# Two more adaLN blocks inside the GLA mixer, unread matmuls in PE's gaps, and jumps ahead of the last waits

## The reference

```
for i in range(4):
    sh1, sc1, g1, sh2, sc2, g2 = split(silu(cond) @ w_ada[i] + b_ada[i], 6)      # adaLN, per group
    h = rmsnorm(x) * (1 + sc1) + sh1
    x = x + g1 * mixer_i(h)     # 0: Hyena (long convolution by DFT), 1: gated linear attention (GLA),
                                # 2: FNet (2-D DFT and a linear map), 3: PoolFormer (window means)
    h = rmsnorm(x) * (1 + sc2) + sh2
    x = x + g2 * moe(h)         # top-1 group of 4, then top-2 of its 4 SwiGLU experts; 16 experts
y = rmsnorm(x)                  # also an output: the final GLA states of the context tokens
```

## Time and profile before

| | |
|---|---|
| median of 3 runs (lowest to highest) | 1424.62 us (1424.25 to 1424.86) |
| profiled execution | 1424.48 us |
| its span, first to last instruction | 1422.3 us |
| PE busy | 1358.9 us, 96% |
| DVE, ACT busy | 360.7 us, 281.8 us |
| read from HBM | 548.98 MB |
| mean granted clock of PE | 0.992 of full speed |
| chain that ended last | PE 83%, DMA 13%, DVE 2%, ACT 1% |

### The profile page before, as it was taken

The page is one execution under the profiler, slowest core; times in us unless marked ns, Lnnn a source line. Parts: engine busy times, 40 slices in busy tenths (PEclk is TensorE's granted clock), DMA queues, the critical chain, the costliest instruction groups (busy, mean ns, idle before and its releaser), DMA issues.

```text
span 1422.3 us, 17398 instructions
## 1 busy us (share of the span) xinstructions
PE 1358.9 (96%) x7294; PEld 748.3 (53%) x7294; DVE 360.7 (25%) x881; ACT 281.8 (20%) x511; POOL 32.1 (2%) x30
## 2 busy tenths in 40 slices
PE   7999999999989999999999989999998898999986
PEld 3786585444435788774444436744443365444433
DVE  3434514111113303323111112331111153111113
ACT  3211024111103221232111104421111053111101
POOL 0001310000000000010000000100000000000000
PEclk9999999999999999999999999999999997999999
DMA  9955999999999993499999999999999999999993
GB/s 382 420 191 214 403 416 394 428 426 428 428 425 421 421 376 102 172 413 403 429 428 426 429 423 420 421 426 428 427 427 428 424 421 425 426 428 428 427 426 153
DMA packets 55076, 552.27 MB, mean 388 GB/s; under 512 B 6033, under 2 KB 8017, under 8 KB 8913
## 3 DMA queue, kind: packets, MB, share of 16 engines
q1 hardware_dynamic: 53360, 549.09, 92.5%
q10 hardware_dynamic: 1634, 2.01, 0.4%
HBM read 548.98 MB, written 2.10 MB: 387 GB/s over the span
## 4 chain that ended last, share of the span: by engine, by line
PE 83%; DMA 13%; DVE 2%; ACT 1%; SPq 0%; issue 0%; POOL 0%; DVEq 0%; POOLq 0%
PE bank L737 26%; PE bank L683 14%; PE bank L761 13%; DMA ring<-in_moe_w 10%; PE bank L643 5%; PE bank L702 5%; PE bank L720 3%; PE bank L514 2%; PE bank L531 2%; DMA ring<-in_pool_w 2%; PE bank L657 2%; PE bank L968 1%; PE bank L860 1%; PE bank L593 1%; PE bank L589 1%; PE bank L744 1%
## 5 line engine op out<-in xcount | busy, mean ns | idle before, releaser
L737 PE MATMUL bank<-ring,arena 128*64 128x512 f32 x896 | 200.4, 595 | 28.1 <-DMA ring<-in_moe_w 26.5
L737 PE MATMUL bank<-ring,hT 128*64 128x512 f32 x1024 | 225.3, 594 | 0.0
L761 PE MATMUL bank<-ring,arena 128*64 128x512 f32 x896 | 198.7, 596 | 0.6 <-DMA ring<-in_moe_w 0.6
L737 PEld LDWEIGHTS bank<-ring,arena 128*64 128x64 f32 x896 | 63.7, 137 | 157.6 <-issue 131.5
L737 PEld LDWEIGHTS bank<-ring,hT 128*64 128x64 f32 x1024 | 72.1, 137 | 139.4 <-issue 137.3
L1447 DVE TENSOR_TENSOR rows<-rows,bank 128x512 f32<-128x512 f32 x32 | 22.0, 688 | 463.6 <-PE bank L737 463.6
L761 PEld LDWEIGHTS bank<-ring,arena 128*64 128x64 f32 x896 | 61.6, 137 | 117.8 <-issue 114.6
L683 PE MATMUL bank<-hT,ring 128*128 128x256 f32 x512 | 112.4, 380 | 0.0
L683 PEld LDWEIGHTS bank<-hT,ring 128*128 128x128 f32 x512 | 96.5, 190 | 15.2 <-issue 2.5
L1167 ACT ACTIVATE yv_big<-bank,arena 128x512 fp32r<-128x512 f32 x64 | 44.0, 688 | 285.5 <-PE bank L761 285.5
L1466 DVE SCALAR_TENSOR_TENSOR yv_rest<-bank,arena,yv_big 128x512 fp32r<-128x512 f32 x64 | 48.1, 751 | 200.6 <-ACT yv_big L1167 200.6
(11 more groups left out here) (217 smaller groups left out, 1281.7 us busy)
## 6 DMA issues: line engine op xcount, KB each, us to landing
ring<-in_moe_w SPq DMA_DIRECT2D x152, 2048.0 KB, 20.4
ring<-in_w_ada SPq DMA_DIRECT2D x96, 1024.0 KB, 22.0
ring<-in_moe_w SPq DMA_DIRECT2D x48, 1024.0 KB, 26.8
arena<-in_moe_w SPq DMA_DIRECT2D x16, 1024.0 KB, 19.6
arena<-in_moe_w SPq DMA_DIRECT2D x8, 2048.0 KB, 11.8
ring<-in_hy_w_in SPq DMA_DIRECT2D x12, 1024.0 KB, 27.3
ring<-in_hy_w_out SPq DMA_DIRECT2D x4, 1024.0 KB, 12.3
ring<-in_gla_w_v SPq DMA_DIRECT2D x4, 1024.0 KB, 22.8
```

The costliest lines, as they stand in the source:

```text
L737: last = mm(bank[4 + kind][SLOTS * e:SLOTS * e + SLOTS, :], x[:, k, at:at + SLOTS], w[:, kk, e, :], start=k == 0, stop=k == KD - 1)
L761: last = mm(bank[6 + q // 2][SLOTS * e:SLOTS * e + SLOTS, :], hidT[:, f, SLOTS * e:SLOTS * e + SLOTS], w[:, ff, e, :], start=f == 0, stop= ...
```

## The change

Blocks 7 and 8 join 5 and 6 inside GLA, between the pieces of the v map, and block 9 takes the place of 7 there; block 10 becomes the one beside layer 1's end, and block 11 is multiplied in FNet. The end of layer 2 and the pool mixer then have no block. Their gaps get `keep_running`: matmuls with `ones` as weights into a PSUM bank of which nobody reads what they write. Such matmuls stand at the start of the kernel too. The loads in `piece_stream` are reordered to match. Three of ACT's four first loads are issued later, behind the first norm's root. The output is stored in four parts instead of two, and SP and ACT jump over `far_rounds` before the last waits and stores. Everything that the reference asks for is still computed. The diff, with little context:

```diff
@@ -125,10 +125,10 @@
     before = [ada(0) + pieces("w_in", 12) + ada(1) + ada(2) + ada(3) + pieces("w_out", 4) + ada(4),
-              ada(5, 0, 5) + pieces("wq", 2) + ada(5, 5) + pieces("wk", 2) + ada(6) + pieces("wv", 4)
-              + pieces("wg", 4) + ada(7) + pieces("wo", 4) + ada(8),
-              ada(9) + pieces("fn", 4) + ada(10),
-              ada(11, 0, 5) + pieces("pool", 1) + ada(11, 5)]
+              ada(5, 0, 5) + pieces("wq", 2) + ada(5, 5) + pieces("wk", 2) + ada(6) + pieces("wv", 2) + ada(7)
+              + pieces("wv", 4)[2:] + ada(8) + pieces("wg", 4) + ada(9) + pieces("wo", 4) + ada(10),
+              ada(11) + pieces("fn", 4),
+              pieces("pool", 1)]
     out, at = [], 0
@@ -467,11 +467,6 @@
-            sp.wait_ge(s("out_ready"), 4)
-            sp.dma_start(a["y"][:, 0:4], hT[:, 0:4]).then_inc(s("stored"), 16)
-            sp.wait_ge(s("state_stored"), 32)
-            sp.wait_ge(s("stored"), 16 * 2)
             def one_round(b, i):
@@ -487,6 +482,11 @@
             far_rounds(sp, "sp", reg, one_round)
+            sp.wait_ge(s("state_stored"), 32)
+            for k in (0, 4):
+                sp.wait_ge(s("out_ready"), k + 2)
+                sp.dma_start(a["y"][:, k:k + 2], hT[:, k:k + 2]).then_inc(s("stored"), 16)
+            sp.wait_ge(s("stored"), 16 * 4)
@@ -522,6 +522,12 @@
             for c in range(4):
+                if c == 1:
+                    ada_turned(6)
+                if c == 2:
+                    ada(7, 0, 8)
+                if c == 3:
+                    ada_turned(7)
                 w8 = arrived(("wv", c), KD)
@@ -532,13 +538,14 @@
                         last.then_inc(s("gla_proj"), 1)
-            ada_turned(6)
+            ada(8, 0, 8)
             gates(pe, 1)
+            ada_turned(8)
             pe.wait_ge(s("v_ready"), 4)
...
-                pe.wait_ge(s("mod_ready"), 7)
+                pe.wait_ge(s("mod_ready"), 9)
                 for m in range(first, end):
@@ -599,7 +606,7 @@
             pe.wait_ge(s("g_raw"), 8)
-            ada(7, 0, 3)
+            ada(9, 0, 3)
@@ -609,8 +616,8 @@
                     last.then_inc(s("osum_mm"), 1)
-            ada(7, 3, 8)
-            residual(1, "wo", oT, lambda k: pe.wait_ge(s("o_ready"), k + 1), turned=7, beside=8)
+            ada(9, 3, 8)
+            residual(1, "wo", oT, lambda k: pe.wait_ge(s("o_ready"), k + 1), turned=9, beside=10)
@@ -852,8 +859,18 @@
+            wide_ones = ones[:, 0:1].broadcast_to([P, 512])
+            def keep_running(times, x, b=7):
+                for _ in range(times):
+                    mm(bank[b][:, 0:x.shape[1]], ones[:], x)
             def moe(i, beside=None):
                 pe.wait_ge(s("rw_loaded"), 16 * (i + 1))
+                if beside is None:
+                    pe.wait_ge(s("mod_ready"), ADAS)
+                    keep_running(2, wide_ones)
                 for k in range(KD):
@@ -876,6 +893,8 @@
                     ada(beside, 6, 7)
+                else:
+                    keep_running(3, wide_ones)
                 pe.wait_ge(s("members"), i + 1)
@@ -885,6 +904,8 @@
                     ada(beside, 7, 8)
+                else:
+                    keep_running(1, wide_ones)
                 pe.wait_ge(s("htok_rest"), 4 * (i + 1))
@@ -906,8 +927,11 @@
+            pe.wait_ge(s("cond_ready"), 1)
+            keep_running(2, ones[:], 0)
             pe.wait_ge(s("filter_loaded"), 16)
             mm(bank[5][0:HY_HID, 0:L], fsmall[0:HY_EMB, 1, 0:HY_HID], fsmall[0:HY_EMB, 0, :]).then_inc(s("f_mm"), 1)
+            keep_running(12, ones[:], 0)
             pe.wait_ge(s("cond_ready"), 3)
@@ -915,6 +939,7 @@
             last.then_inc(s("f_mm"), 1)
+            keep_running(3, ones[:], 0)
             norm(0)
@@ -1010,12 +1035,12 @@
             pe_gla(pe, arrived, ada, ada_turned, norm, h_ready, project, residual)
-            moe(1, 8)
-            ada(9, 0, 2)
+            moe(1, 10)
+            ada(11, 0, 2)
             norm(4)
-            ada(9, 2, 5)
+            ada(11, 2, 5)
             pe.wait_ge(s("cm_loaded"), 16 * 2)
@@ -1030,7 +1055,7 @@
                     last.then_inc(s("mix_mm"), 1)
-            ada(9, 5, 8)
+            ada(11, 5, 8)
             pe.wait_ge(s("mix_rows"), 8)
@@ -1040,15 +1065,14 @@
                     last.then_inc(s("mix_mm"), 1)
-            ada_turned(9)
+            ada_turned(11)
             pe.wait_ge(s("mix_rows"), 8 + 4)
-            residual(2, "fn", rhs=fnm, beside=10)
-            moe(2, 10)
-            ada(11, 0, 2)
+            residual(2, "fn", rhs=fnm)
+            moe(2)
             norm(6)
-            ada(11, 2, 5)
+            keep_running(2, wide_ones)
             pw = arrived(("pool", 0), KD)
@@ -1061,14 +1085,12 @@
                         last.then_inc(s("mix_mm"), 1)
-            ada(11, 5, 8)
             pe.wait_ge(s("mix_rows"), 12 + 4)
...
                 last.then_inc(s("res_mm"), 1)
-            ada_turned(11)
             norm(7)
@@ -1094,10 +1116,7 @@
-            act.dma_start(base[:], a["c_base"]).then_inc(s("base_loaded"), 16)
-            act.dma_start(ar(19472, 3 * P), a["c_masks"]).then_inc(s("masks_loaded"), 16)
             act.dma_start(skip_row[0:1], a["skip"]).then_inc(s("skip_loaded"), 16)
-            act.dma_start(rw[:], a["router"][0]).then_inc(s("rw_loaded"), 16)
@@ -1232,6 +1251,9 @@
             inverse_root(0)
+            act.dma_start(base[:], a["c_base"]).then_inc(s("base_loaded"), 16)
+            act.dma_start(ar(19472, 3 * P), a["c_masks"]).then_inc(s("masks_loaded"), 16)
+            act.dma_start(rw[:], a["router"][0]).then_inc(s("rw_loaded"), 16)
             for c in range(10):
@@ -1362,9 +1384,10 @@
-            act.wait_ge(s("out_ready"), 8)
-            act.dma_start(a["y"][:, 4:8], hT[:, 4:8]).then_inc(s("stored"), 16)
             far_rounds(act, "act", reg, one_round)
+            for k in (2, 6):
+                act.wait_ge(s("out_ready"), k + 2)
+                act.dma_start(a["y"][:, k:k + 2], hT[:, k:k + 2]).then_inc(s("stored"), 16)
@@ -1764,8 +1787,9 @@
             v.memset(sc[:], 0.0).then_inc(s("sc_clear"), 1)
-            ada_rows(6)
-            ada_mod(6)
+            for n in (6, 7, 8):
+                ada_rows(n)
+                ada_mod(n)
             scores(0)
@@ -1786,15 +1810,15 @@
                 tt(o, o, ors[:, m // 2], ALU.mult).then_inc(s("o_ready"), 1)
-            ada_rows(7)
+            ada_rows(9)
             residual(1, g1(1))
-            ada_mod(7)
-            moe(1, 8)
+            ada_mod(9)
+            moe(1, 10)
             norm(4)
-            ada_rows(9)
+            ada_rows(11)
             residual(2, g1(2))
-            ada_mod(9)
-            moe(2, 10)
+            ada_mod(11)
+            moe(2)
             norm(6)
@@ -1802,14 +1826,12 @@
             chain(tt(xT[:], xT[:], gb.unsqueeze(3).broadcast_to([P, KD, G, L]), ALU.add))
-            ada_rows(11)
             for m in range(KD):
...
                 last.then_inc(s("x_added"), 1)
-            ada_mod(11)
             moe(3)
```

## The result

Four executions of the changed kernel took 1412.62 to 1415.59 us, median **1413.8 us**; the kernel before took 1424.74 us beside it (1424.25 to 1425.24). The ratio is 0.9923, 95% interval 0.9908 to 0.9938: faster by 0.8%. The forecast was 1413.5 us. Of the terms behind it some were wrong and cancelled, so the stages come first. From here on "the changed kernel" is the one of the diff.

A forecast was written before the change was run, and what follows sets the result against it. PE, busy for 96% of the span, sets the end with its few idle stretches. Terms -3.3 + 15.3 - 1.3 - 6.5 - 8.7 - 3.4 - 3.2 = -11.1 from 1424.6 give 1413.5 us, range 1406 to 1420.5.

The forecast's parts named there:

- GLA: Gated mixer: two more blocks, their turnings and a new modulation wait, no wait for loads; +15.3 us.
- a granted clock of under 1.00 behind the pool mixer: Layer 3: named as a sign that the forecast is wrong; clock forecast at 1.00 in every window behind 12 us.
- a wait of PE for a load between 500 and 545: In GLA: PE idling on loads there was named as a sign of being wrong; 0 to 2 us possible, 0 taken.
- Start: First norm: unread products raise the clock (-2.4), three loads leave the queue ahead of x (-0.9); sum -3.3 us.
- Layer 2: Mixer and routing chain of layer 2: block work leaves, mostly from gaps; -1.3 us.
- MoE 2 and 3: Expert stages of layers 2 and 3: eight fewer loads ahead, longer lead; -6.5, and -3.4 plus -1.9 for layer 3's first gathers.
- (d): Removed loads do not shorten the MoEs, as SP's ordered queue hands the lead back; 1423.4 us, 8 in 100.
- (e): The MoE tails vanish altogether, 201.2 and 200.9 instead of 205.0 twice, a further -8; 1405.5 us, 8 in 100.
- Layer 3: Layer 3's mixer and routing: block 11 leaves and the clock is kept; -8.7 us, of which -1.9 is the first gathers.
- Rival (b): The clock still falls in the last routing chain, layer 3, costing 4.9 us; 1418.4 us, 11 in 100.
- Rival (c): Unread products hold the clock nowhere; layer 2's chain and the pool mixer fall too; 1434 us, 5 in 100.
- End: Last stores: jump moved into SP's idle time (2.5 us), store of half the size (-0.7); sum -3.2 us.

The follow-up runs named there:

- e5: The changed kernel once more, unaltered: median 1413.49 us, ratio 0.9923 to the kernel before.
- e4: The changed kernel with base, masks and router loaded ahead of x again, as in the kernel before: 1415.42 us, ratio 0.9934.
- e6: The changed kernel with only one block more in GLA instead of two, block 11 back in layer 2's end and beside its experts: 1413.35 us, ratio 0.9917.
- e8: The changed kernel with eight expert slabs of layer 2 queued ahead of the first w2 loads: 1415.66 us, ratio 0.9936.
- e1: The kernel before with only the adaLN blocks moved, no unread products, old start and end: 1430.91 us, ratio 1.0041.
- e3: The changed kernel without the unread products of layers 2 and 3, those of the start kept: 1423.83 us, ratio 0.9992.
- e11: The changed kernel without the two unread products behind norm(6), ahead of the pool mixer: 1414.45 us, ratio 0.9925.
- e2: The kernel before with only the new start (unread products, later loads) and new end (jumps, four stores), no block moved: 1418.33 us, ratio 0.9952.
- e7: The changed kernel with block 11's pieces only where PE waits, replacing layer 2's unread products: 1411.8 us, ratio 0.9899.
- e9: e7 plus three half-width unread products in layer 3's bare gaps: 1409.7 us, ratio 0.9889.
- e12: The changed kernel without the 17 unread products of the start, the three loads still behind x: 1414.8 us, ratio 0.9921.

## Why the forecast held

That the sum came within 0.3 us of the median is partly luck. The stages fell by 9.7 us in the profiled execution and by 12.6 in e5, for a forecast of 11.1: GLA's +1.1 and layer 3's +2.1 were made up for by the two MoEs (-1.2 and -0.8), and layer 3 alone moves by 2.6 us from one execution to the next. Two things that the prediction named as signs of being wrong came true: a granted clock of under 1.00 behind the pool mixer, and a wait of PE for a load between 500 and 545. Both were small, 2.6 and 0.4 us.

**Start.** Right in sum (-3.3; -3.2 in the profiled execution, -2.6 in another), wrong in its parts. "I take -0.9, bounds 0 and -1.0" for the loads: x came 2.2 us earlier, outside the bounds, so the size over the full rate (0.43 MB at 424 GB/s) is not what these small loads cost there. Why is not shown; in before the engines moved 134 to 380 GB/s at first, until near 6 us. (The rule of the Trainium skill that the prediction cites, "DMA: Bandwidth & Descriptors", section "Issuing engines are not separate DMA queues", agrees in kind: loads of ScalarE's queue do delay those of SyncE's. It gives no price for it.) "-2.4" for the clock: 2.0 by itself (e4), and about 1.0 remains once x is early, since the unread products stand in PE's order ahead of x.

**GLA.** +15.3, measured +16.4: two blocks at 7.0 and 7.7 (0.4 of it the wait for the last piece, where "0 to 2 us of waiting; I take 0" was the forecast), two turnings 0.9, and 0.3 for the modulation; the last 0.5 I can't place.

**Layer 2.** -1.3, measured -1.1.

**MoE 2 and 3.** -6.5 and -5.3, measured -7.7 and -6.1. The mechanism, eight loads fewer and so a longer lead capped by the ring, is shown by e6 (eight loads back: MoE 2 219.2 us, 218.7 before) and e8 (a longer lead is of no use). The forecast lead, 33 us, was met. The cap is at 204.2 rather than 205.0. Rivals (d) and (e) are out: PE still waits 18.2 us for slabs over the four stages (26.5 before), 6.1 us in the first and 3.6 to 4.5 in each of the others.

**Layer 3.** -6.8; -4.7 in the profiled execution, -7.3 in e5 (from the norm's sum to the first expert product 19.4 and 16.8 us, forecast 17 to 18). Rival (b), the clock falls all the same, happened in part: the mean clock shows it in three of ten executions, and in the profiled one it lasted 6.8 us and cost 2.6 instead of 4.9 us, as it was over before the gathers. "So I take the clock as kept" was right for most executions.

**Rival (c)**, that unread products don't hold the clock, is out, but what it says of layer 2 is true: without any of them, and with the old start and end, the change gives 1430.9 us (e1), without those of layers 2 and 3 alone 1423.8 (e3). I had put the price of the clock at 4.9 us a chain; e3 against e5 gives 6.6 and 6.2. The "up to 8" for the pool mixer was too much: its clock was down for about 3 us in e1 and in e11, and e11 lost 0.6 us there.

**End.** -3.2, measured -2.9: 2.4 from the jump (drain 0.2 instead of 2.6 us behind the last landing), 0.5 from the store, which landed in 3.6 instead of 4.1 us. That the size did this is not shown: in e1, which has the old end, stores of the full size landed in 3.4 to 3.7 us.

So the gain of 10.9 us is not that of the moved blocks. Start and end are 6.9 us of it (e2); moving the blocks loses some 6 us by itself (e1), and pays only because the freed chains are then filled with matmuls that do nothing (10 us, e3). And the move of a second block is worth nothing even then (e6). Fewer, better placed pieces (e7) and full gaps (e9) give 1409.7 us, which is faster than both kernels: the interval of its ratio ends at 0.9904, that of the changed kernel begins at 0.9907 or 0.9908.

## What to carry to other kernels

When real work is taken out of a chain of small steps, price what the clock does there as well as the work: here it decided between +6 us (e1) and -4 us (the changed kernel against e2). Spread real work over such gaps before unread work; filling the small gaps too cost nothing here and may have helped. Work moved off a stage that waits for its loads gains through the loads that go with it; ask whether the buffer's places cap the lead before counting on more. Two edits that bring the same waiting instruction forward don't add up: find what is ready second.

## What the runs showed of the hardware

- Behind an idle stretch of PE of 2.2 us, with logits and transposes after it, the granted clock was 0.50 for 20 us (e1). The mean clock of e3 was 0.984 to 0.988 in each of its twelve executions, that of the changed kernel 0.996 to 0.999 in ten. Followed by the pool mixer's 64 larger matmuls, such a gap cost about 3 us at half clock (e11).
- The clock could also fall in the midst of busy work: at 1179.1 us in the changed kernel, with gaps of no more than 0.7 us in the 20 us ahead, for 6.8 us. It came in some executions of the same kernel and not in others, and once in layer 2, for 6 us, behind gaps of 1.2 and 0.5 us (e12).
- Over the first 18 us the profile gave a granted clock of 1.00 while the same products took 1.94 us in one kernel and 1.07 in another (before and the changed kernel): at the start of a kernel durations tell more than that row.
- Three loads of 98, 192 and 128 KB on another queue ahead of a 1 MB load delayed its landing by 2.2 us (9.30 against 7.10; 9.0 to 10.0 against 7.1 to 8.3 over all traces), twice their size over the full rate.
- Taking a pause of the loads away (338 to 420 GB/s over 30 us) changed nothing in the stage behind it (207.0 and 207.4 us).
- From the landing of the last store to SP's drain it took 2.6 us with the jump between the two, and 0.2 us with the jump ahead of the last wait.
